# Broadcasting rows on TensorE: plain f32 matmuls in place of transposes of a broadcast column, in a two-model transformer kernel

## The reference

```python
# first block, layer 0 (gated delta rule)
q = jnp.repeat(l2_norm(q), rep, axis=2)          # 8 heads of 128, used by 16
k = jnp.repeat(l2_norm(k), rep, axis=2)
g = jnp.cumsum(g, axis=-1)                       # in chunks
diff = g[..., :, None] - g[..., None, :]
decay = jnp.where(tril, jnp.exp(jnp.where(tril, diff, 0.0)), 0.0)
a = jnp.where(strict, jnp.einsum("bhncd,bhnjd->bhncj", k_beta, k) * decay, 0.0)
t_inv = lax.linalg.triangular_solve(eye + a, ...)
# second block, layer l
mod = cond @ ada_w[l] + ada_b[l]
sh1, sc1, g1, sh2, sc2, g2 = jnp.split(mod, 6, axis=-1)
x = x + g1 * (y @ w_out[l])
x = x + g2 * _conv_glu_ffn(h, ...)
```

## Time and profile before

| | |
|---|---|
| Median of 3 runs | 1616.7 us (1607.62 to 1625.02) |
| The profiled execution's own time | 1616.7 us |
| Its span | 1614.9 us |
| PE (matmuls) busy | 1522.4 us, 94% |
| DVE busy | 1079.1 us, 67% |
| ACT busy | 880.5 us, 55% |
| POOL busy | 394.2 us, 24% |
| Mean granted clock of TensorE | 0.971 |

### The profile page before, as it was taken

One profiled execution on the slowest core, in us unless ns is written; L12 is line 12 of the kernel. 1 busy time (PEld: TensorE's weight loads), 2 busy tenths in 40 slices (PEclk: granted clock), 3 DMA queues, 4 the chain that ended last, 5 costly groups with the idle time before them and its releaser, 6 DMA issues.

```text
span 1614.9 us, 35254 instructions
## 1 busy us (share of the span) xinstructions
PE 1522.4 (94%) x15260; PEld 1383.6 (86%) x15260; DVE 1079.1 (67%) x1792; ACT 880.5 (55%) x1452; POOL 394.2 (24%) x271
## 2 busy tenths in 40 slices
PE   7999988999999989999999888999999989999999
PEld 6988987789998878999878777899988768799987
DVE  5765463458789676777987755776647665676664
ACT  7663663454443655644456645566636664566652
POOL 0233371424434000344311330012200131012220
PEclk9999999999999989999999988999999997999999
DMA  7322232249888342788953202555452400445550
GB/s 286 131 107 81 80 107 107 80 143 368 334 324 342 120 182 79 290 325 320 351 200 124 86 30 78 230 188 183 160 180 77 146 28 28 190 176 183 183 183 27
DMA packets 40187, 275.89 MB, mean 171 GB/s; under 512 B 4576, under 2 KB 4832, under 8 KB 8672
## 3 DMA queue, kind: packets, MB, share of 16 engines
q1 hardware_dynamic: 40032, 273.63, 46.0%
HBM read 272.57 MB, written 1.05 MB: 169 GB/s over the span
## 4 chain that ended last, share of the span: by engine, by line
PE 79%; DVE 8%; ACT 8%; issue 3%; POOL 1%; DMA 1%; ACTq 0%; SPq 0%; POOLq 0%
PE ps L552 22%; PE ps L554 21%; PE ps L553 21%; PE ps L560 4%; DVE wl L540 2%; PE ps L565 2%; ACT wh L532 2%; PE ps L2185 1%; DMA ring<-in_ws 1%; DVE ring L928 1%; DVE hTl L709 1%; ACT ps L771 1%; DVE x_sb L2998 0%; PE ps L2012 0%; PE ps L2560 0%
## 5 line engine op out<-in xcount | busy, mean ns | idle before, releaser
L540 DVE TENSOR_TENSOR wl<-ring,wh 128x1024 fp32r<-128x1024 f32 (+5 forms) x376 | 473.3, 1266 | 305.3 <-ACT wh L532 303.7
L532 ACT ACTIVATE wh<-ring 128x1024 fp32r<-128x1024 f32 (+4 forms) x428 | 436.9, 1027 | 410.1 <-PE ps L554 404.4
L552 PE MATMUL ps<-hTh,wh 128*128 128x256 f32 (+1 forms) x1912 | 549.3, 287 | 7.7 <-DVE hTl L709 3.5
L554 PE MATMUL ps<-hTh,wl 128*128 128x256 f32 (+1 forms) x1912 | 542.9, 284 | 0.0
L553 PE MATMUL ps<-hTl,wh 128*128 128x256 f32 (+1 forms) x1912 | 541.0, 283 | 1.8 <-issue 1.8
L552 PEld LDWEIGHTS ps<-hTh,wh 128*128 128x128 f32 (+1 forms) x1912 | 363.4, 190 | 12.8 <-DVE wl L540 5.8
L553 PEld LDWEIGHTS ps<-hTl,wh 128*128 128x128 f32 (+1 forms) x1912 | 363.0, 190 | 2.2 <-issue 2.0
L554 PEld LDWEIGHTS ps<-hTh,wl 128*128 128x128 f32 (+1 forms) x1912 | 360.5, 189 | 0.1
L548 POOL TENSOR_TENSOR wl<-ring,wh 128x1024 fp32r<-128x1024 f32 x52 | 142.7, 2744 | 350.1 <-ACT wh L532 350.1
L1484 DVE SCALAR_TENSOR_TENSOR arena<-arena 128x1024 f32<-128x1024 f32 x96 | 160.9, 1692 | 0.6 <-DMA arena<-in_ws 0.6
L552 PE MATMUL ps<-wh,acts 128*128 128x512 f32 x366 | 145.2, 397 | 0.8 <-DVE wl L540 0.8
(11 more groups left out here) (463 smaller groups left out, 2097.2 us busy)
## 6 DMA issues: line engine op xcount, KB each, us to landing
ring<-in_ws SPq DMA_DIRECT2D x197, 1024.0 KB, 5.0
arena<-in_ws SPq DMA_DIRECT2D x48, 1024.0 KB, 8.4
ring<-in_ws SPq DMA_DIRECT2D x5, 768.0 KB, 4.5
ring<-in_ws SPq DMA_DIRECT2D x4, 512.0 KB, 3.5
ring<-in_ws SPq DMA_DIRECT2D x2, 780.0 KB, 4.3
rowt<-in_rowp SPq DMA_DIRECT2D x2, 610.0 KB, 3.9
x_sb<-in_x SPq DMA_DIRECT2D x2, 512.0 KB, 4.8
arena<-in_rowp SPq DMA_DIRECT2D x2, 512.0 KB, 5.9
```

What stands on the lines that cost most here:

```text
L532: ac.act(unit_hl(u)[0], unit_src(u), ACT.Copy).then_inc(*W.a(("hi", u)))
L540: ve.tt(l, unit_src(u), h, OP.subtract).then_inc(*W.v(("lo", u)))
L552: pe.mm(o_, lh, rh, start=start, stop=False)
L554: return pe.mm(o_, ll, rh, start=False, stop=stop)
```

## The change

Row broadcasts are made in another way in three places.

In `qknorm`, each half first transposes `qrs` as a whole (two transposes, 128 tokens by 16 heads each, to 16 rows of 256 tokens in bank 7), DVE copies that to a new SBUF tile `rT`, and each `bc` step is then two plain f32 matmuls with 16 rows: a column of the identity, repeated 128 times, picks the head's row of `rT`, which moves with 256 columns. `qrs` is set to 1 once before the first half, since the first transposes also read the heads that the second half writes. In `decay`, the transposes become plain matmuls that pick a head's row of `gcT` (16 rows, 128 columns). In `gate_t`, the same operands as before go through a plain matmul instead of a transpose.

```diff
+        rT = al(256)
...
         def qknorm_t(pe):
             for half in range(2):
+                yield "rT", half
+                pe.wait_ge(*GP.v["qrs", half])
+                if half:
+                    pe.wait_ge(*GP.a["ktok", 0])
+                for t in range(2):
+                    m = tr(pe, psum[7][0:16, 128 * t:128 * t + 128], qrs.rearrange("p (t n) -> p t n", t=2)[:, t, :])
+                m.then_inc(*GP.t(("rT", half)))
                 for i in range(4 * half, 4 * half + 4):
                     yield "bc", i
-                    pe.wait_ge(*GP.v["qrs", half])
-                    if i == 5:
-                        pe.wait_ge(*GP.a["ktok", 0])
+                    pe.wait_ge(*GP.v["rT", half])
                     if i % 4 >= 2:
                         pe.wait_ge(*GP.v["qn", i - 2])
                     for j in range(2):
                         f = 2 * QKORDER[i] + j
-                        for t in range(2):
-                            m = tr(pe, qn_bank(i)[:, 256 * j + 128 * t:256 * j + 128 * t + 128], bc(qrs[:, 16 * t + f:16 * t + f + 1], [128, 128]))
+                        m = pe.mm(qn_bank(i)[:, 256 * j:256 * j + 256], bc(C["ident"][0:16, f:f + 1], [16, 128]), rT[0:16, :], start=True, stop=True)
...
+                if half == 0:
+                    ve.zero(qrs, 1.0).then_inc(*GP.v("qrs1"))
+                    ve.wait_ge(*GP.v["qrs1"])
+                else:
+                    ve.wait_ge(*GP.t["rT", 0])
...
+                yield "rTv", half
+                ve.wait_ge(*GP.t["rT", half])
+                if half:
+                    ve.wait_ge(*GP.t["bc", 3])
+                ve.cp(rT[0:16, :], psum[7][0:16, 0:256]).then_inc(*GP.v(("rT", half)))
...
+        idr = lambda hh: bc(C["ident"][0:16, hh:hh + 1], [16, 128])
...
             for t in T2:
-                pe.wait_ge(*GP.v["gc"])
+                pe.wait_ge(*GP.v["gcT", 1])
...
                 for h in H4:
-                    m = tr(pe, bank[t][:, h, :], bc(gc[:, t, 4 * sg + h:4 * sg + h + 1], [128, 128]))
+                    m = pe.mm(bank[t][:, h, :], idr(4 * sg + h), gcT[0:16, 128 * t:128 * t + 128], start=True, stop=True)
...
                 for k in range(4):
                     c = (16, 40)[i] + 4 * n + k
-                    m = tr(pe, psum[(2, 4)[i] + n][:, 128 * k:128 * k + 128], bc(MC(l)[:, c:c + 1], [128, 128]))
+                    m = pe.mm(psum[(2, 4)[i] + n][:, 128 * k:128 * k + 128], bc(MC(l)[:, c:c + 1], [128, 128]), C["ident"], start=True, stop=True)
...
-            *[(10.4 + 8 * h, 0.2, of("qn", [("mean", h), ("sqrt", h), ("rec", h)])) for h in range(2)],
+            *[(10.4 + 8 * h, 0.2, of("qn", [("mean", h), ("sqrt", h), ("rec", h), ("rT", h), ("rTv", h)])) for h in range(2)],
```

## The result

| | before | after |
|---|---|---|
| median of 6 runs, us | 1617.82 | 1638.13 |
| lowest and highest, us | 1607.62, 1625.02 | 1626.87, 1642.05 |
| profiled execution: span, us | 1614.9 | 1632.8 |
| its mean granted clock | 0.971 | 0.973 |

What follows compares the result with a forecast made beforehand. PE (TensorE) was taken as the bound. Added PE work 12.2 us plus hand-over waits 3.1 less 3.0 taken back by existing waits gave +12.3, so 1616.7 + 12.3 = 1629.0 us; range 1616 to 1637.

Steps and rivals of the forecast that it cites:

- Which engine sets the end: Whole kernel: PE sets the end, busy 1522.4 of 1614.9 us; the other engines mostly wait for it.
- Rival 1: GDN stage: its added time mostly vanishes in waits, leaving the gate and some of decay; +5, 1622 us; chance 0.22.
- The price of a broadcast transpose, and of matmuls with 128 rows: decay, gate, qknorm: 0.109 us per removed transpose; 0.235 per plain f32 matmul of 128 columns, bounds 0.224 and 0.25.
- Fewer rows bring nothing. I take 0.45: qknorm's bc: 16-row matmuls with 256 columns are no cheaper than 128-row ones, 0.45 us each, pairs about 0.9.
- Rival 4: New matmuls: the broadcast operand is slow to read, so they cost twice the price; +24, 1641 us; chance 0.06.
- The hand-over waits: qknorm: PE waits for reciprocals before transposing qrs, then for DVE's copy before bc; 3.1 us over both halves, bounds 0 and 4.
- What existing waits take back: PE's existing waits in qknorm, the first inverse and decay absorb 3.0 us of the added time, bounds 1 and 7.
- The clock set to nothing outside rival 2: Whole kernel: the sum of +12.3 us held no term for more time at PE's lower clock.
- rival 2: qknorm: hand-over stalls pull PE's clock to half in both halves, with upper prices; +17 + 2, 1636 us; chance 0.13.
- Rival 3: PE's clock: removing transposes, if counted as less work, keeps it up; faster, 1612 us with half the low stretches gone; chance 0.06.
- theory C: From the follow-ups, not the prediction: PE's clock falls where its time goes into transposes or few-row matmuls, not by delay.
- The signs named: Right: gate groups 1.9 us, bc pairs 0.9, four waits, stage to 350 us +8. Wrong: early low clock, stage over +20.

Runs made afterwards that it cites:

- the hand-over alone: Kernel before plus only qknorm's transposes of qrs, DVE copy to rT, memset and waits; bc broadcasts stay transposes: 1615.71 us, ratio 1.0012.

## Why the prediction was wrong in size

**Which engine sets the end: right.** PE's chain carried the loss, and the edits add up, as they do where one queue is the bound. Rival 1 (mostly swallowed) fell.

**The price of a broadcast transpose, and of matmuls with 128 rows: right.** The gate costs 0.224 each where 0.235 was taken and the lower bound was 0.224.

**"Fewer rows bring nothing. I take 0.45": failed.** Fewer rows cost more. The neighbour on which this rested was the pair L2446 of the earlier trace rows with 4 rows and 0.53 each; I read it as "not cheaper" and then took the price of 128-row neighbours. The 16-row pairs cost 1.06 to 1.15 (0.53 to 0.58 each), and `decay` 0.26 each, above the bound of 0.25. Ahead of a group with 16 rows there is a further 0.09 us that the way of pricing didn't see. With both, the added work is 3.7 for the gate, 5.2 for `decay`, 6.4 for `bc` and 0.4 for qrs: 15.7 where 12.2 stood, so 3.5 us too little. Rival 4 had the size of this at `bc` but a wrong cause: the broadcast operand is in both versions, and with 128 rows the matmuls with it cost 0.223 each, no more than the 0.224 of those without it. Its sum was also wrong: at twice the price the new matmuls give 64 x (0.47 - 0.109) + 16 x 0.90 - 3.5 + 0.4 = 34 us and a time of 1651, not +24 and 1641. That the measured 1638 is near its 1641 means nothing.

**The hand-over waits: right in place and cause, 3.1 forecast and 2.3 measured.** The largest difference is at the second pair of transposes, 0.8 where 1.3 was reckoned; in the trace of the hand-over alone this wait is 1.18 in its bracket and in after 0.66, so it moves from trace to trace.

**What existing waits take back, 3.0: partly seen, its worth not settled.** PE's waits at `bc` 3 (0.81 us), and at the first inverse (0.64) are gone in after, and one of the last `decay` gave up 0.51. By the table the `qknorm` edit (10.7 summed, 9.2 measured) and `decay` (12.5 and 11.0) leave 1.5 us each that could be taken back, and the whole change nothing. All of that is within the errors.

**The clock set to nothing outside rival 2: this step failed, and it is the larger one.** The sum 12.3 has no term for it. After ran 102.4 us of low clock in the mean of its 43 executions, the kernel before 83 to 88. At 0.36 that is 5 to 7 us. Work 15.7, waits 2.3 and clock about 6 make 24, less what of the 3.0 is really taken back; measured were +20.3 between the medians of six and +23.5 in the longer count. Rival 2 had the mechanism but the wrong trigger, so that its 1636 came near the measured 1638 by luck. The hand-over alone (86.8) shows nothing in the clock, and `decay` alone does it (107.9). The low stretch from 68 to 79 us in the trace of `qknorm` alone, which has the hand-over and the 16-row pairs, is the sign that rival 2 named; no other trace has it. For the rest of the stage the forecast looked only at the two waits near 220 us, which drew no low stretch in the three microseconds around them. The right look would have been the stage as a whole: a mean of 0.98 over 318 us in before says that the stage had low stretches to multiply.

**Rival 3 (removed transposes keep the clock up): not in the whole.** The Trainium skill's page "TensorE: Matmul & The Clock Gate" (Part 4, PE-mode transpose) says that transposes do not count as busy PE in the same way. The doubled transposes (108.8) against 128-row matmuls of about the same added time (89.8) agree with it, with an error of 6 on the difference, and so does the gate alone, which has 10 us less low clock than before. The change had no profit from that, since matmuls with 16 rows cost the clock as much (107.9).

**What stays open.** Two things are shown: the `decay` edit adds low-clock time, and with 128 rows instead of 16 the cost beyond the work is gone. Extra transposes of the old kind do what the 16-row matmuls do. All of this is theory C. Against it stand the 3.8 us of dense matmuls behind `decay`, which cost +9.3 in the mean of three kernels, although nothing in them uses the array little. The traces lean to C, one execution of each kernel. The same window over the stage is at 0.95 with doubled transposes, but at 0.97, 0.98 and 0.97 with the dense matmuls (within `decay`, behind it, and behind it again; the first three follow):

```profile
57.00:375.00 318.00, 296.62 (x5443) 272.32 (x5442) 166.27 (x317) 165.74 (x270) 112.49 (x83) 0.95 0.29 104
```

```profile
57.00:375.00 318.00, 296.61 (x5468) 272.17 (x5467) 169.27 (x321) 168.77 (x273) 113.73 (x84) 0.97 0.28 104
```

```profile
57.00:375.00 318.00, 293.12 (x5462) 268.50 (x5461) 167.47 (x320) 167.76 (x272) 113.60 (x84) 0.98 0.29 103
```

So in the traces dense work, wherever it stands, took less of the clock in the stage than transposes or 16-row matmuls did. Why dense work behind `decay` costs more than itself stays open. And in `qknorm` the rows made no difference to the clock that shows: +4 us of low clock with 16 rows, +8 with 128. One experiment was not made: a kernel with an idle pause of the same length in place of the added work would have separated delay from work.

**The signs named.** The gate's groups (1.8), all four waits and the absence of new low stretches between 57 and 110 us (clock 1.00 in its window) came as written; the pairs (1.1, not 0.9) and the stage (19 us, not 8) did not. "More than 20 us in the stage" was named as what would prove the sum wrong. It stopped just short of that.

None of the versions run beats the kernel before. The best form of the idea is the gate alone or `decay` with 128 rows, each 3 us slower in the mean, by intervals that reach down to no change.

## What to carry to other kernels

Here a broadcast by a plain f32 matmul cost at least twice one by a transpose (0.224 against 0.109 us at 128 columns and 128 rows, more with few rows); where PE is the bound, it needs a saving elsewhere that is worth more. Take the price of a matmul with few rows from a neighbour with few rows, by start-to-start times that begin at the matmul ahead of it, not by the duration of its record. And where a stage's mean clock is below 1, an edit of a few microseconds there can cost twice its own length or more (11.0 us for 5.2 of work in `decay`): give the clock a term of its own in the sum, read from the window over the whole stage, and compare mean clocks over many executions before any cause is named.

## What the runs showed of the hardware

- f32 matmuls with 128 moving columns took 0.26 us with 16 rows and with 32, and 0.223 with 128. Pairs with 256 columns took 1.06 to 1.15 us with 16 rows and 0.86 with 128. Ahead of a group with 16 rows there was 0.21 us from start to start in place of the pace of 0.12. The Trainium skill's page "TensorE: Matmul & The Clock Gate" (Why this matters for your kernels) gives a single matmul of 32 rows the same time as one of 128. Here, in a stream where each matmul has weights of its own, it is 17% more, and the measurement decides. The same page (LDWEIGHTS) gives a weight load of 32 rows the time of one of 128, and the loads' records agree, first after with 16 rows and then `decay` with 128 rows:

```profile
L1093 PEld LDWEIGHTS ps<-small,cst x64: 180/185/328, 84.3 to 235.7; 16*128 16x128 f32 x64
```

```profile
L1080 PEld LDWEIGHTS ps<-small,cst x64: 185/190/338, 80.2 to 222.5; 128*128 128x128 f32 x64
```

  So the records of neither loads nor matmuls show the difference; only the pace does.
- 3.5 to 3.8 us of added work on PE in the GDN stage cost between 3.4 us (`decay` with 128 rows) and 11.4 us (dense matmuls behind it), and those that cost 6.9 us or more have 10 to 21 us more low-clock time.
- Filling PE's idle time with dense matmuls ahead of the last `decay` did not raise the clock: 91.6 us of low-clock time against 88.3.
